# Decode attention in a fused trunk layer: key products one slot earlier, exponentials over two slots, sums behind the last value tile

## The reference, cut to what matters

```python
z = xn @ p['w_in']                      # queries, keys, values, inputs of the other mixers
# for each of the 8 batches, 16 heads:
#   s = q @ keys.T * scale, over 1280 cached rows (and the 8 new ones), with a mask of multiplicities
#   p = exp(s - max(s));  o = (p @ values) / sum(p)
mixed = concat([rmsnorm(o_att), rmsnorm(y_ssm), rmsnorm(y_conv)])
x = x + mixed @ p['w_out']
x = x + (silu(rms(x) @ p['w_gate']) * (rms(x) @ p['w_up'])) @ p['w_down']
```

## Time and profile before

| | us |
|---|---|
| median of three runs | 1550.64 |
| lowest and highest | 1546.78, 1552.99 |
| the profiled execution | 1547.88 |
| its span in the trace | 1546.1 |

### The profile page before, as it was taken

One profiled execution on the slowest core, in us unless ns is written; L12 is line 12 of the kernel. 1 busy time (PEld: TensorE's weight loads), 2 busy tenths in 40 slices (PEclk: granted clock), 3 DMA queues, 4 the chain that ended last, 5 costly groups with the idle time before them and its releaser, 6 DMA issues.

```text
span 1546.1 us, 27979 instructions
## 1 busy us (share of the span) xinstructions
PE 1495.4 (97%) x11431; PEld 1430.1 (92%) x11431; DVE 841.6 (54%) x1086; ACT 597.7 (39%) x883; POOL 218.6 (14%) x317
## 2 busy tenths in 40 slices
PE   9999898998888999999999999999999999999997
PEld 8999776776677899999999999999999999999997
DVE  6669798874465767544444444444444433333434
ACT  6333433434654445333333333333333333333332
POOL 7873344310260000000000000000000000000100
PEclk9999998999999999999999999999999999999999
DMA  7645797998679444444444444444444444444443
GB/s 263 190 169 188 281 364 268 364 342 325 257 296 371 138 164 150 149 150 149 148 149 148 150 147 149 148 150 148 147 150 150 148 151 149 151 148 151 150 150 109
DMA packets 93271, 296.41 MB, mean 192 GB/s; under 512 B 9728, under 2 KB 11008, under 8 KB 92800
## 3 DMA queue, kind: packets, MB, share of 16 engines
q1 hardware_dynamic: 92608, 294.10, 54.7%
q10 hardware_dynamic: 576, 1.08, 0.2%
HBM read 289.06 MB, written 5.43 MB: 190 GB/s over the span
## 4 chain that ended last, share of the span: by engine, by line
PE 84%; DVE 9%; ACT 3%; DMA 2%; issue 2%; SPq 0%; DVEq 0%; ACTq 0%
PE ps L2070 20%; PE ps L2071 20%; PE ps L2072 20%; PE ps L1916 5%; PE ps L1918 2%; PE ps L1954 2%; PE ps L1960 2%; PE ps L1955 2%; DVE wlo L1029 2%; DMA kv<-in_cv 2%; PE ps L1751 2%; PE ps L1767 2%; PE ps L2023 1%; PE ps L2022 1%; PE ps L2021 1%
## 5 line engine op out<-in xcount | busy, mean ns | idle before, releaser
L1382 DVE TENSOR_TENSOR wlo<-raw,whi 128x1024 fp32r<-128x1024 f32 x264 | 325.2, 1232 | 519.9 <-ACT whi L906 519.8
L906 ACT ACTIVATE whi<-raw 128x1024 fp32r<-128x1024 f32 x264 | 279.9, 1060 | 606.2 <-PE ps L2072 601.7
L2072 PE MATMUL ps<-xh,wlo 128*128 128x320 f32 x1400 | 432.6, 309 | 0.0
L2070 PE MATMUL ps<-xh,whi 128*128 128x320 f32 x1400 | 432.6, 309 | 0.0
L2071 PE MATMUL ps<-xl,whi 128*128 128x320 f32 x1400 | 432.6, 309 | 0.0
L2070 PEld LDWEIGHTS ps<-xh,whi 128*128 128x128 f32 x1400 | 262.8, 188 | 0.0
L2071 PEld LDWEIGHTS ps<-xl,whi 128*128 128x128 f32 x1400 | 262.8, 188 | 0.0
L2072 PEld LDWEIGHTS ps<-xh,wlo 128*128 128x128 f32 x1400 | 262.8, 188 | 0.0
L2070 PE MATMUL ps<-hh,whi 128*128 128x320 f32 x696 | 215.1, 309 | 0.0
L2071 PE MATMUL ps<-hl,whi 128*128 128x320 f32 x696 | 215.1, 309 | 0.0
L2072 PE MATMUL ps<-hh,wlo 128*128 128x320 f32 x696 | 215.1, 309 | 0.0
(11 more groups left out here) (336 smaller groups left out, 1837.2 us busy)
## 6 DMA issues: line engine op xcount, KB each, us to landing
raw<-in_w_gu SPq DMA_DIRECT2D x176, 512.0 KB, 3.3
raw<-in_w_dn SPq DMA_DIRECT2D x88, 512.0 KB, 3.4
raw<-in_w_in SPq DMA_DIRECT2D x78, 512.0 KB, 5.2
kv<-in_cv SPq DMA_DIRECT2D x61, 512.0 KB, 8.2
kv<-in_ck SPq DMA_DIRECT2D x32, 768.0 KB, 7.0
kv<-in_ck SPq DMA_DIRECT2D x32, 512.0 KB, 7.5
raw<-in_w_out SPq DMA_DIRECT2D x32, 512.0 KB, 3.4
raw<-in_cv SPq DMA_DIRECT2D x19, 512.0 KB, 8.0
```

What stands on the lines that cost most here:

```text
L906: act.activation(whi[:, j % SPL, :], raw[:, j % RAW, :], ACT.Copy).then_inc(S["w_hi"], 1)
L1382: v.tensor_tensor(wlo[:, j % SPL, :], raw[:, j % RAW, :], whi[:, j % SPL, :].bitcast(F32), ALU.subtract) \
L2070: t_.matmul(out, whi[:, slot, w], ah[:, k, :], start=(k == 0), stop=False)
L2072: last = t_.matmul(out, wlo[:, slot, w], ah[:, k, :], start=False, stop=(k == 2 * units - 1))
```

## The change

Each batch begins one slot earlier (every sixth slot from 36). The exponentials are split: two in step 4, two in step 5. The transpose `turn_probabilities` stays in its slot (now step 6), but moves in VectorE's program from behind `low` to the front, ahead of `mask_scores`, which now serves the next batch's step 0 in that slot. The sums of the probabilities go from a step of their own in bank 6 to a spare column of bank 4, right behind the last value tile; their reciprocal goes to that slot as well, and `scale_output` one slot later, ahead of `move_output`. On TensorE `turn_output` comes after the scores and values of its slot. The value tiles keep their slots (43 to 47 for batch 0 and so on).

```diff
-START_OF = (37, 43, 49, 55, 61, 67, 73, 79)
-TURN, VALUES, OUTPUT = 5, 6, 11
+START_OF = (36, 42, 48, 54, 60, 66, 72, 78)
+TURN, VALUES, OUTPUT = 6, 7, 12
+V_STEPS = (0, 0, 1, 1, 2, 2, 3, 3, 4, 4)
+def value_slot(b, j):
+    return START_OF[b] + VALUES + V_STEPS[j]
...
-            for b in batches(s, TURN):
-                end.append((6, ("norm", b)))
...
-            def exponent(b):
+            def exponent(b, groups):
                 act.wait_ge(S["s_bias"], 4 * b + 4)
-                for g in range(4):
+                for g in groups:
...
                 for b in batches(s, OUTPUT):
+                    scale_output(b)
                     if b >= LATE:
                         move_output(b)
-                for b in batches(s, VALUES + 4):
-                    scale_output(b)
...
-                    exponent(b)
+                    exponent(b, (0, 1))
+                for b in batches(s, 5):
+                    exponent(b, (2, 3))
...
-                v.reciprocal(rsum[:, b:b + 1], ps[:, 6, 0:1]).then_inc(S["s_sum"], 1)
+                v.reciprocal(rsum[:, b:b + 1], ps[:, 4, 2 * P:2 * P + 1]).then_inc(S["s_sum"], 1)
...
+                for b in batches(s, TURN):
+                    turn_probabilities(b)
                 for step_ in range(KS):
                     for b in batches(s, step_):
                         mask_scores(b, step_)
...
-                for b in batches(s, TURN):
-                    turn_probabilities(b)
+                for b in batches(s, VALUES + 4):
                     inverse_sums(b)
...
-                fill(6, "norm", b)
...
+                if j == KEY_TILES - 1:
+                    sum_probabilities(b)
...
             def end(s):
 
+                for step in range(KS):
+                    for b in batches(s, step):
+                        scores(b, step)
+                for b in range(DEC_BATCH):
+                    for j in range(KEY_TILES):
+                        if value_slot(b, j) == s:
+                            values(b, j)
                 for b in batches(s, OUTPUT):
                     if b >= LATE:
                         turn_output(b)
-                for step in range(KS):
-                    for b in batches(s, step):
-                        scores(b, step)
-                for b in batches(s, TURN):
-                    sum_probabilities(b)
```

More of the change, by code:

```diff
@@ L469, in build @@
             here = [("k", b, NP * i + part) for i in range(KS) for b in batches(s, i) for part in range(NP)]
-            here += [("v", b, j) for b in range(DEC_BATCH) for j in range(KEY_TILES) if START_OF[b] + VALUES + j // 2 == s]
+            here += [("v", b, j) for b in range(DEC_BATCH) for j in range(KEY_TILES) if value_slot(b, j) == s]
             KV_ORDER += here
@@ L515, in released @@
                     "score": lambda: ("s_masked", KS * key[1] + key[2] + 1) if key[2] < KS - 1 else ("new_masked", key[1] + 1),
-                    "norm": lambda: ("s_sum", key[1] + 1),
                     "late": lambda: ("late_added", key[1] + 1)}[kind]()
@@ L1760, in sum_probabilities @@
                 for g in range(4):
-                    last = t_.matmul(ps[32 * g:32 * g + 32, 6, 0:1], fold[:], psums[:, b, g:g + 1], start=True, stop=True,
+                    last = t_.matmul(ps[32 * g:32 * g + 32, 4, 2 * P:2 * P + 1], fold[:], psums[:, b, g:g + 1], start=True, stop=True,
                                      tile_position=(0, 32 * g))
```

## The result

The changed kernel takes 1539.25 us (median of 7 runs, 1534.89 to 1540.77), the kernel before 1550.64 in the same session: a ratio of 0.9932, 95% interval 0.9912 to 0.9951. That is 11.4 us faster, 0.7%. The forecast was 1526 us, 24.6 us faster. The time lies in the range, but under half of the forecast gain came.

The account below looks back on a forecast made before the run. TensorE, 97% busy, was taken as the bound, losing time to the sums' waits and half clock. Gains of 16.4 + 0 + 3.9 + 2.8 = 23.1 us took 1547.88 to 1524.8, median put at 1526; range 1515 to 1542 us.

Parts of the forecast that it names:

- The three signs of being wrong: Clock falling more than twice, slots 42 to 65 over 160 us, or TensorE waits for scores or `wlo` there.
- The sums' waits go: TensorE's 20.5 us of waits ahead of the probability sums vanish, and with them what the clock loses.
- What is late next, the cap of slots 42 to 65: VectorE at 95% busy limits these slots to 151.9 us, from 168.3: 16.4 us gained, between 8 and 21.8.
- The rival of the stage bound by VectorE and transfers: TensorE's removed waits return at `wlo`, mask or value tiles; 1539.6 us, or up to 1546; chance 0.15.
- The transpose costs nothing: On VectorE ahead of `low`, covered by `wlo`'s slack: 0 us; without cover, 2 us for each of 8 batches.
- The waits at the turning: TensorE's `turn_output` waits for scaling behind the copy of `whi`: 0.3 to 4.4 us in slots 60 to 90.
- These waits charged with no clock: New `turn_output` waits of 2.2 to 4.4 us bring no clock fall, judged from one 3.17 us value-tile wait.
- Slots 66 to 83 even: New turning waits there balance the old waits that go: 0 us, between +4 and -6.
- Slot 84 and after: Wait of 4.94 and 3.4 us of clock go, 4.4 of turning waits come: +3.9 us, between 0 and 8.
- The value tiles: Half of TensorE's two longest waits for value tiles, slots 70 and 75, goes: +2.8 us, between 0 and 5.6.
- The other rivals: Late transpose makes TensorE wait for `wlo`, 1558 us, chance 0.09; sums' waits partly stay through bank 6, 1535, chance 0.06.
- The case in which everything is won: Rival: 21.8 us gained in slots 42 to 65 and the better bounds after: 1516 us, chance 0.06.

Follow-up runs that it names:

- r7: e1 with the two products of the scan's part 3 left out on VectorE from slot 42 to 65, so later states are wrong; 1509.35 us.
- r9: e1 with each transpose of the probabilities issued twice, 1.64 us more of VectorE for each of 8 batches; 1532.99 us.
- e1: The changed kernel with the scaling of the output moved ahead of the copy of `whi` in ScalarE's slot; 1521.57 us.
- u1: The changed kernel with the scaling ahead of the copy of `whi` for the last two batches only; 1532.30 us, ratio 0.9898 to the kernel before.
- e2: The changed kernel with four exponentials in step 4 again and the transpose of batches 1 to 7 at the end of VectorE's slot before; 1543.70 us.

## Why the prediction was too high by half

By its own steps, in the profiled executions: 23.1 us were forecast and 8.6 came. Of the 14.5 missing, 9.5 are in slots 42 to 65, 2.4 from slot 84 on, 2.8 are the value tiles (the stretches ahead of 42 and from 66 to 83 give +0.3 and -0.1).

The three signs of being wrong that the prediction named all came: five falls of the clock, 161.4 us for slots 42 to 65, and longer waits of TensorE at the scores and a new one for `wlo` there.

- *The sums' waits go*: right, 20.5 to 1.4 us. In ScalarE's program two exponentials, then `whi`, stand in slots 40 and 41, as said.
- *What is late next, the cap of slots 42 to 65*: this is the step that failed. I let VectorE be 95% busy throughout, as in one stretch of before, and got 151.9 us. Its work stayed (144.52 to 145.26), but its share came to 145.26 / 161.41 = 90%, from 94% in the first stretch to 85% in the third (38.92 of 45.94). The third shows why a best share can't be spread over stretches: VectorE runs without a gap up to slot 55 while TensorE waits 1.02 and 4.08 us for it, the clock falls, and then TensorE at half speed lets VectorE wait. r7 and r9 show the bound itself, from both sides: 18.7 us less of VectorE in these slots give 12.2, 6.4 more cost 7.2, the clock's part included. The rival of the stage bound by VectorE and transfers had the mechanism for this part, VectorE's half of it; that the transfers bind it as it stands fell with r7. Its time, 1539.6 us, is the measured one, but by luck: it gave 4.4 us to slots 42 to 65, which gave 6.9, and 3.9 to the end, which gave 1.5.
- *The transpose costs nothing*: not borne out. Its cover was `wlo`'s slack in a slot that is on time, but where it decides, in slots 54 and 55, VectorE is late. Behind a late transpose it is the mask that TensorE needs first, for bank 6, and not `wlo`. r9 prices one more transpose there at its full length or more. No run puts the transpose back behind `low`, so what its move alone cost stays open.
- *The waits at the turning*: right in place, cause and size, 14.9 us in all against 14.7. Slots 60, 66, 72, 78, 84 and 90 had 0.7, 2.0, 2.8, 4.6, 2.4 and 2.4 where 0.3, 2, 3.6, 4.4, 2.2 and 2.2 were said. ScalarE's timeline in slot 84 has the copies named in the earlier trace rows, one behind the other:

```profile
484.98 1.04 ACT L688 ACTIVATE whi<-raw 128x1024 fp32r<-128x1024 f32 x1
485.93 0.49 ACT L781 ACTIVATE ah<-z,vec 128x256 fp32r<-128x256 f32 x1
486.33 0.46 ACT L747 ACTIVATE osb<-ps,rsum 128x256 f32<-128x256 f32 x1
```

- *These waits charged with no clock*: wrong, and the second failed step. The clock fell behind those of slots 72 and 84 and within that of slot 78, and e1 and u1 show that these falls go with the waits. It did not fall behind those of 60, 66 and 90. The Trainium skill, "TensorE: Matmul & The Clock Gate", section "HAM oscillation", has as its example waits for transfers of some 3 to 5 us between bursts. The prediction applied it to each of the new waits, from 2 us on. The trace doesn't bear out that form (three of six waits brought a fall), but falls came with waits shorter than that, 2.77 and 2.41 us, so the one row that I put against the rule was no ground to charge nothing. An estimate of what the windows cost is half of TensorE's busy time in them: 21.02 / 2 = 10.5 us, where it was 24.89 / 2 = 12.4 before and the forecast had them gone. Of the 10.5, the three at the turning are (3.41 + 6.30 + 3.41) / 2 = 6.6.
- *Slots 66 to 83 even*: right, 149.43 and 149.53, but only as a balance. The old waits and those for value tiles (the 2.8 us that I had put on top) went, and 9.35 us of turning with two falls took their place (1.99 + 2.77 + 4.59). e1, which takes the turning's waits away, wins 11.9 us there.
- *Slot 84 and after*: 1.5 us in place of 3.9, short mostly by the window at 487.14 (1.7 us) and the 0.4 us by which the two waits were longer.
- *The value tiles*: 8.3 to 1.9 us of waits for transfers, more than the 2.8 counted; by the last two points nothing of it is left in the time.
- The other rivals: the wait does not go through VectorE to `wlo` (1.02 us in all), and none of it stayed at the sums.
- *The bounds*: two of its sums don't come out. The case in which everything is won, by the bounds given, is 21.8 + 4 + 8 + 5.6 = 39.4 us, 1508 and not 1516; and the worse bounds add up to a gain of 2 us, not 10. Neither decided the result.

Open is why the clock falls after one such wait and not after another of the same length: 1.93 us in slot 63 did, 2.22 in e1 in the same slot did not; 2.41 in slot 84 did, 2.43 in slot 90 did not. So is whether slots 42 to 65 can be made faster by moving VectorE's work to ScalarE, which is busy 66 of their 161 us; that was not tried.

The fastest kernel that computes all is e1: 1521.57 us, 29 us under the kernel before, of which the change as made gives 11 and the scaling's place 18.

## What to carry to other kernels

When a wait is moved to another operation, look at what stands ahead of that operation's input in the producer's queue: here one scaling of 0.46 us, put behind a copy that itself waits for the consumer, cost 17.7 us of a gain of 29, clock included, and a move of one line gave it back. Where an engine is the bound behind the waits, don't take its best stretch as the cap for all: work out for each slot whether it can be on time, and where it can't, count an instruction at the head of its queue at its full length. A fall of the clock behind a new wait of TensorE goes into the range as a possible cost: here 2.41 us had one behind it and 2.43 us had none.

## What was not expected of the hardware

The clock windows came back to the same sum, 27.32 and 27.30 us, though 20.5 us of waits were taken away and 14.9 us of others came. That the sums are equal is chance: it is 20.49 in u1, 6.83 in e1 and 30.71 in e2. With less work on VectorE the transfers moved the same data at 377 and 363 GB/s in slots 48 to 59, where the kernel after has 351 and 315: a share of 0.95 was no sign that they were the bound.
